# Another offset for the split weights in each of the seven stages that multiply h

## What is computed

```python
def swiglu(h, w_in, w_down):
    a, b = jnp.split(h @ w_in, 2, axis=-1)
    return (jax.nn.silu(a) * b) @ w_down
...
h = rms_norm(x, norm_g[layer, 0]) * (1.0 + scale) + shift
x = x + 0.5 * gate * swiglu(h, ffn_w_in[layer, 0], ffn_w_down[layer, 0])
h = rms_norm(x, norm_g[layer, 1]) * (1.0 + scale) + shift
y = diff_attention(h, ...) if layer == 0 else hgrn2(h, ...)      # both begin with h @ w, end with @ w_o
x = x + gate * y
h = rms_norm(x, norm_g[layer, 2]) * (1.0 + scale) + shift
x = x + 0.5 * gate * swiglu(h, ffn_w_in[layer, 1], ffn_w_down[layer, 1])
...
p = rmsnorm(x, norm_g_2) @ w_in_2                                # the last layer, one product of h for all mixers
```

## Time and profile before

| | |
|---|---|
| median of 3 runs | 2407.84 us (2407.11 to 2408.68) |
| span of the profiled execution | 2407.3 us |
| TensorE matmul, busy | 2373.9 us, 11034 instructions |
| TensorE weight load, busy | 1906.8 us, 11034 instructions |
| VectorE, busy | 1273.2 us |
| ScalarE, busy | 860.6 us |
| GpSimd, busy | 202.0 us |
| granted TensorE clock, mean | 0.994 of full speed |

### The profile page before, as it was taken

One profiled execution on the slowest core, in us unless ns is written; L12 is line 12 of the kernel. 1 busy time (PEld: TensorE's weight loads), 2 busy tenths in 40 slices (PEclk: granted clock), 3 DMA queues, 4 the chain that ended last, 5 costly groups with the idle time before them and its releaser, 6 DMA issues.

```text
span 2407.3 us, 30397 instructions
## 1 busy us (share of the span) xinstructions
PE 2373.9 (99%) x11034; PEld 1906.8 (79%) x11034; DVE 1273.2 (53%) x1953; ACT 860.6 (36%) x1320; POOL 202.0 (8%) x337
## 2 busy tenths in 40 slices
PE   7999999999999999999999999999999999999998
PEld 5888888677788888888888888888888888867766
DVE  6886334455678873343333355555533333469554
ACT  4222223566543222242222243344422222344443
POOL 1212000000001110000000013331000000120200
PEclk9999999999999999999999999999999999999999
DMA  8899332321259973223333321212233333242211
GB/s 279 277 287 294 111 96 72 98 62 53 70 168 288 289 230 108 86 79 96 96 99 108 90 79 54 62 53 79 86 97 96 96 111 96 69 97 62 62 53 53
DMA packets 420385, 285.27 MB, mean 119 GB/s; under 512 B 22690, under 2 KB 397788, under 8 KB 420304
## 3 DMA queue, kind: packets, MB, share of 16 engines
q1 hardware_dynamic: 397888, 207.64, 29.8%
q0 software_dynamic: 20896, 73.80, 9.3%
q10 hardware_dynamic: 1520, 2.77, 0.3%
HBM read 281.85 MB, written 6.72 MB: 120 GB/s over the span
## 4 chain that ended last, share of the span: by engine, by line
PE 92%; DVE 3%; ACT 2%; DMA 1%; issue 1%; SPq 1%; POOL 0%; ACTq 0%; DVEq 0%; POOLq 0%
PE bank L686 13%; PE bank L688 13%; PE bank L687 13%; PE bank L863 7%; PE bank L861 7%; PE bank L862 7%; PE bank L1530 4%; PE bank L1532 4%; PE bank L1531 4%; PE bank L1557 2%; PE bank L721 2%; PE bank L723 2%; PE bank L722 2%; PE bank L1179 1%; PE bank L1152 1%; PE bank L701 1%
## 5 line engine op out<-in xcount | busy, mean ns | idle before, releaser
L642 DVE TENSOR_TENSOR w_lo<-raw,w_hi 128x1024 fp32r<-128x1024 f32 (+1 forms) x331 | 434.0, 1311 | 423.9 <-ACT w_hi L623 418.4
L623 ACT ACTIVATE w_hi<-raw 128x1024 fp32r<-128x1024 f32 (+1 forms) x331 | 369.7, 1117 | 478.0 <-PE bank L688 243.2
L686 PE MATMUL bank<-h_hi,w_hi 128*128 128x512 f32 x1344 | 523.4, 389 | 1.6 <-DVE w_lo L642 1.6
L687 PE MATMUL bank<-h_lo,w_hi 128*128 128x512 f32 x1344 | 523.3, 389 | 0.0
L688 PE MATMUL bank<-h_hi,w_lo 128*128 128x512 f32 x1344 | 523.2, 389 | 0.0
L686 PEld LDWEIGHTS bank<-h_hi,w_hi 128*128 128x128 f32 x1344 | 252.4, 188 | 54.5 <-DVE w_lo L642 2.4
L687 PEld LDWEIGHTS bank<-h_lo,w_hi 128*128 128x128 f32 x1344 | 252.4, 188 | 52.4
L688 PEld LDWEIGHTS bank<-h_hi,w_lo 128*128 128x128 f32 x1344 | 252.4, 188 | 52.3
L861 PE MATMUL bank<-g_hi,w_hi 128*128 128x512 f32 x704 | 274.5, 390 | 0.0
L863 PE MATMUL bank<-g_hi,w_lo 128*128 128x512 f32 x704 | 274.1, 389 | 0.0
L862 PE MATMUL bank<-g_lo,w_hi 128*128 128x512 f32 x704 | 274.1, 389 | 0.0
(11 more groups left out here) (420 smaller groups left out, 3021.7 us busy)
## 6 DMA issues: line engine op xcount, KB each, us to landing
raw<-in_ffn_w_in SPq DMA_DIRECT2D x176, 512.0 KB, 3.9
ada<-in_ada_w POOLq DMA_DIRECT2D x128, 512.0 KB, 5.0
raw<-in_ffn_w_down SPq DMA_DIRECT2D x64, 704.0 KB, 4.6
raw<-in_hgrn_w_in SPq DMA_DIRECT2D x32, 512.0 KB, 4.0
raw<-in_attn_w_qkv SPq DMA_DIRECT2D x24, 512.0 KB, 3.8
raw<-in_w_in SPq DMA_DIRECT2D x22, 512.0 KB, 3.8
ada_first<-in_ada_w SPq DMA_DIRECT2D x16, 512.0 KB, 10.7
bias_scratch<-bias_lines POOLq DMA_DIRECT2D x14, 320.0 KB, 9.0
```

The source lines that it names most:

```text
L623: line(nc.scalar.activation(w_place(n, 0, k * P)[0], raw[:, n % 4, 0:k * P], ACT.Copy), hi_ready)
L642: line(nc.vector.tensor_tensor(lo, raw[:, n % 4, 0:k * P], hi.bitcast(F32), ALU.subtract), lo_ready)
L686: nc.tensor.matmul(out_ap, wh, xh, start=(k == 0), stop=False)
L687: nc.tensor.matmul(out_ap, wh, xl, start=False, stop=False)
```

## The change

Seven stages get a place of their own inside the slots. A table gives each an offset in elements: 16 (F0), 32 (F1), 48 (F2), 64 (F3), 80 (QKV), 96 (HIN), 112 (P2), that is 64, 128, 192, 256, 320, 384 and 448 bytes. Both halves of a block, in `w_hi` and in `w_lo`, are written and read that much further on; 1024 + 112 elements fit a slot of 1408. `raw`, h, the 16 blocks of each feed-forward that multiply g, and WO, HO and OUT stay where they are. No instruction is added, removed or moved on any engine, and no wait changes: the instruction lists of the two kernels read alike but for the line numbers.

```diff
+        PLACED = {"F0": (UP, 16), "F1": (UP, 32), "F2": (UP, 48), "F3": (UP, 64), "QKV": (24, 80), "HIN": (32, 96),
+                  "P2": (len(SECOND), 112)}
+
+        def w_cols(n, a, b):
+
+            at = sum(o for name, (count, o) in PLACED.items() if FIRST[name] <= n < FIRST[name] + count)
+            return slice(at + a, at + b)
 
         def w_place(n, a, b):
...
-            return w_hi[:, n % 2, a:b], w_lo[:, n % 2, a:b]
+            return w_hi[:, n % 2, w_cols(n, a, b)], w_lo[:, n % 2, w_cols(n, a, b)]
...
-                line(nc.scalar.activation(w_hi[:, n % 2, HALF:KD * P], raw[:, n % 4, HALF:KD * P], ACT.Copy), hi_ready)
+                line(nc.scalar.activation(w_hi[:, n % 2, w_cols(n, HALF, KD * P)], raw[:, n % 4, HALF:KD * P], ACT.Copy),
+                     hi_ready)
...
-                    nc.tensor.matmul(banks[b][:, :], w_hi[:, s, k * P:(k + 1) * P], xh, start=(k == 0), stop=False)
+                    nc.tensor.matmul(banks[b][:, :], w_hi[:, s, w_cols(n, k * P, (k + 1) * P)], xh, start=(k == 0),
+                                     stop=False)
...
-                wh, wl = w_hi[:, n % 2, k * P:(k + 1) * P], w_lo[:, n % 2, k * P:(k + 1) * P]
+                wh, wl = w_place(n, k * P, (k + 1) * P)
```

More of the change, by code:

```diff
@@ L573, in first_half_hi @@
             act.wait_ge(half_used, m + 1)
-            line(nc.scalar.activation(w_hi[:, n % 2, 0:HALF], raw[:, n % 4, 0:HALF], ACT.Copy), half_hi)
+            line(nc.scalar.activation(w_hi[:, n % 2, w_cols(n, 0, HALF)], raw[:, n % 4, 0:HALF], ACT.Copy), half_hi)
         def first_half_lo(dve, line, m):
@@ L579, in first_half_lo @@
             dve.wait_ge(half_hi, m + 1)
-            line(nc.vector.tensor_tensor(w_lo[:, n % 2, 0:HALF], raw[:, n % 4, 0:HALF],
-                                         w_hi[:, n % 2, 0:HALF].bitcast(F32), ALU.subtract), half_lo)
+            line(nc.vector.tensor_tensor(w_lo[:, n % 2, w_cols(n, 0, HALF)], raw[:, n % 4, 0:HALF],
+                                         w_hi[:, n % 2, w_cols(n, 0, HALF)].bitcast(F32), ALU.subtract), half_lo)
         IN_H = {FIRST["WO"] + 2: 0, FIRST["WO"] + 3: 1}
+        PLACED = {"F0": (UP, 16), "F1": (UP, 32), "F2": (UP, 48), "F3": (UP, 64), "QKV": (24, 80), "HIN": (32, 96),
[3 more added lines that the diff above has]
+            return slice(at + a, at + b)
         def w_place(n, a, b):
@@ L631, in split_lo @@
             if n in HALVED:
-                line(nc.vector.tensor_tensor(w_lo[:, n % 2, HALF:KD * P], raw[:, n % 4, HALF:KD * P],
-                                             w_hi[:, n % 2, HALF:KD * P].bitcast(F32), ALU.subtract), lo_ready)
+                line(nc.vector.tensor_tensor(w_lo[:, n % 2, w_cols(n, HALF, KD * P)], raw[:, n % 4, HALF:KD * P],
+                                             w_hi[:, n % 2, w_cols(n, HALF, KD * P)].bitcast(F32), ALU.subtract), lo_ready)
                 return
@@ L700, in product_pair @@
                     s = (n + b) % 2
-                    nc.tensor.matmul(banks[b][:, :], w_hi[:, s, k * P:(k + 1) * P], xh, start=(k == 0), stop=False)
-                    nc.tensor.matmul(banks[b][:, :], w_lo[:, s, k * P:(k + 1) * P], xh, start=False, stop=False)
+                    nc.tensor.matmul(banks[b][:, :], w_hi[:, s, w_cols(n, k * P, (k + 1) * P)], xh, start=(k == 0),
+                                     stop=False)
+                    nc.tensor.matmul(banks[b][:, :], w_lo[:, s, w_cols(n, k * P, (k + 1) * P)], xh, start=False,
+                                     stop=False)
                 pe.wait_ge(h_ready, KD * m + k + 1)
@@ L705, in product_pair @@
                     s = (n + b) % 2
-                    last = nc.tensor.matmul(banks[b][:, :], w_hi[:, s, k * P:(k + 1) * P], xl, start=False,
+                    last = nc.tensor.matmul(banks[b][:, :], w_hi[:, s, w_cols(n, k * P, (k + 1) * P)], xl, start=False,
                                             stop=(k == KD - 1))
@@ L735, in product_rows @@
                     xh, xl = h_hi[:, k, t * P:(t + 1) * P], h_lo[:, k, t * P:(t + 1) * P]
-                    wh = w_hi[:, n % 2, k * P:k * P + width]
-                    wl = w_lo[:, n % 2, k * P:k * P + width]
+                    wh, wl = w_place(n, k * P, k * P + width)
                     nc.tensor.matmul(o, xh, wh, start=(k == 0), stop=False)
@@ L1955, in out_part @@
                 hi, lo = y_pair(k)
-                wh, wl = w_hi[0:r, n % 2, k * P:(k + 1) * P], w_lo[0:r, n % 2, k * P:(k + 1) * P]
+                wh, wl = (w[0:r] for w in w_place(n, k * P, (k + 1) * P))
                 nc.tensor.matmul(B[j % 2][:, :], wh, hi[0:r], start=(m == 0), stop=False)
```

## The result

The changed kernel takes 2424.21 us (median of 3 runs, 2421.12 to 2426.09) against 2407.84 before: a ratio of 1.0063, 95% interval 1.0044 to 1.0083. It is slower, by 0.6% and clear of the interval, where no change was forecast. The span of its profiled execution is 2422.6 us, 15.3 more than before.

A forecast was written before the change was run, and what follows sets the result against it. TensorE was taken to bound the kernel through the pitch of its matmuls. Split 0, load 0 and pitch 0 on the profiled 2407.3 us, with the median 0.5 us above the span, gave 2407.8 us; range 2393 to 2437.

The forecast's parts named there:

- What bounds the kernel, and the scale: TensorE: time is matmul count times pitch; 6240 matmuls have moved weights, one ns on each pitch is 6.2 us.
- Writing the weights, 0: Split on ACT and DVE: another write address adds 0 to 0.5% of 1.236 us, hidden behind TensorE; taken as 0.
- loading them, 0: TensorE's weight load: 188 ns under a 227 ns pitch, no longer from another address; taken as 0.
- Weights and h at the same time, 0: TensorE reading weights and stream at a new distance within 512 bytes: settled pitch of 0.2267 us kept; taken as 0.
- The bounds: Limits on the pitch change of the 6240 matmuls: +0.0067 and -0.0067 us each, +41.6 and -41.6 us in all.
- Slower: h and weights fall out of step: Rival on TensorE's pitch: settled rhythm lost, about half the matmuls at 0.233 us, +22 us, 2430 us; chance 0.37.
- Faster: the present distance is itself the bad one: Rival on TensorE's pitch: 0.220 us in two feed-forwards, -14 us, 2394 us; in all seven stages 2366; chance 0.22.
- Mixed: Rival: the seven offsets act both ways and cancel to within 4.8 us; counted under no change, chance 0.41.
- The Trainium skill's rule: TensorE pitch of N / 2.4 GHz plus about 2.5 ns; would give 68 us less, 2339 us, placed among the rivals.
- The range: Kernel time expected to hold 8 in 10: 2393 to 2437 us, about 0.08 left above and 0.11 below.

The follow-up runs named there:

- e1: Changed kernel with weights 64 bytes further on in all seven stages; 2441.38 us, ratio 1.0143 to the kernel before.
- e2: Changed kernel with weights 256 bytes further on in all seven stages; 2408.06 us, ratio 1.0000 to the kernel before.
- e4: Changed kernel with weights of all seven stages and both halves of h 64 bytes further on; 2408.01 us, ratio 1.0000 to the kernel before.
- e5: Changed kernel with weight offsets 16, 32, 48, 8 bytes in F0 to F3, zero in QKV, HIN, P2; 2431.15 us against 2408.39 before.
- e7: Changed kernel with halves apart: w_lo alone moved 64, 128, 192 bytes in F0 to F2, w_hi alone 64 in F3; 2424.66 us.
- e8: Changed kernel using 64, 64, 32, 32 weight columns in `product`, F0 to F3, offsets 64, 0, 0, 64 bytes; 2428.18 us against 2408.39 before.
- e9: Changed kernel with h_lo moved 64 bytes, weight halves hi/lo at 0/64, 0/0, 64/64, 0/192 bytes in F0 to F3; 2434.83 us against 2409.24 before.

## Why the prediction was wrong

**What bounds the kernel, and the scale: right.** Nothing but the pitch of the 6240 matmuls changed, and the groups and waits stayed. The time follows from the pitch by stage, as worked out below.

**Writing the weights, 0; loading them, 0: right.** 1236, 1055 and 188 ns again. The transposes that were taken as rows for another address showed no difference, and rightly for the load itself.

**Weights and h at the same time, 0: this step failed.** The text took 0 because "the row nearest to a stage with one fixed offset is the settled stretch", where the distance does not change from matmul to matmul. It took constancy of the distance for the condition of the short pitch. e1 has one constant distance in each stage and runs at 233.3 ns; e2 and e4 have another one and run at 226.7. The value of the distance counts, modulo 256 bytes. Zero was a special case that the trace of before couldn't show as one, since every long stretch in it had it. For the measured value it was y8, the one tile with another distance (-192 bytes, so 64 modulo 256), that was near: 0.233 us. That row was read, put in the bounds, and set aside since its neighbours were as slow. Taken to the ns they were not quite: the three matmuls of y8 take 700 to 702 ns in seven of OUT's eight blocks, the three of the tile in front of it 691 to 697, and in the first block, where y8 takes 691, "every time" doesn't hold.

**The bounds held:** +6.67 ns was the step in F0, and no stage's pitch fell. By stage, 6.67 ns x 1056 = 7.0 us in F0 (the table has 6.2, since TensorE pauses less there than before), 5.7 x 1056 = 6.0 in F1, 2.2 x 1056 = 2.3 in F2, 0 in F3, together 15.3; QKV, HIN and P2 add 2.3, and the part ahead of F0, which the change does not touch, is 1.5 shorter (it lasts 39.1 to 41.0 us in the profiles of e1 to e4). The -0.9 of the last row says nothing: with no offset in P2 it lasts 313.9 to 314.9 us in e5 to e7 and 315.4 before.

**The rivals.** *Slower: h and weights fall out of step* was the case, at 2430 us for 2424. That its size came near was luck: it let the odd multiples of 64 bytes pay the full step and the even ones nothing. In fact 192 bytes cost a third of a step, 128 nearly a whole one, and 256 nothing. It also said that the broken stages would pay as the others do; they paid 2.3 us for 2016 matmuls, 1.1 ns each. That much of them is unsettled anyway is the likely reason, not shown. *Faster: the present distance is itself the bad one* falls: of twelve distances zero is the best for 512 columns. *Mixed* is answered by the windows: no feed-forward gained.

The Trainium skill's rule weighed there (page "TensorE: Matmul & The Clock Gate", section "Wait — 56ns, not 53.3ns?", 215.7 ns for 512 columns) was reached by no arrangement; the shortest pitch for 512 was 226.7, and for 496 columns 220.0. The same page, section "Step-by-step: what each phase is for", says that loading the next weights doesn't take read bandwidth from the running matmul. By that the size of the load would not matter to the pitch; in e8 it did, and in both directions (a quarter of the load: 231.7 for 226.7 ns at distance zero, 231.7 for 233.3 with 64 bytes). That the places of the two matter to each other, 226.7 against 233.3 ns, the page does not say.

**The range** held the time (2393 to 2437). The chance for slower, 0.37, was too low for a row that had been seen.

## What to carry to other kernels

In fp32r products where each matmul loads its own weights and streams 512 columns, allocate so that weight tiles and streamed tiles begin at the same place modulo 256 bytes, both halves of a split alike; here each of the eleven other distances tried cost 1.7 to 6.7 ns a matmul, up to 1.4% of the kernel, and halves placed apart 4.4 to 7.7. For other lengths of the stream measure it: with 480 columns 64 bytes were 0.7 ns better than zero. When something has a single value in the whole trace, the trace can't tell what other values cost; the one odd tile that differs is then the best row there is, and deserves the weight. Measure a pitch over a long window by its count, and look at single starts only for the rhythm.

## What the runs showed of the hardware

- The pitch of a settled run of fp32r matmuls closes on a beat of 6.67 ns, mostly within seven matmuls (fifteen in F1 of e9, 522 beats), for 384 to 512 columns and at every distance tried. In the kernel before, the starts of all settled stretches, taken modulo 6.667 ns, lie on one straight line over the whole execution (it drifts by 3.7 ns in 2.4 ms, no stretch is off by more than 0.3): the beat runs on through the pauses between them. In e4, with h and its weights 64 bytes further on and g and its weights not, the stretches with g lie on such a line and those with h on a second one, 1.7 ns off it, a quarter of a beat; with the weights of h moved by 256 bytes (e2) there is one line again. So the beat is tied to where the operands lie, and a quarter of it for a quarter of 256 bytes fits the 256 bytes after which the pitches repeat. What beats is not known.
- After other work a run of such matmuls needs up to ten to settle, at distance zero in the kernel before; until then single pitches go from 224 to 237 ns, 232 on the mean in the earlier trace rows.
- Fewer weight columns shortened the recorded load (188, 134 and 109 ns for 128, 64 and 32) and not, as a rule, the pitch: 32 instead of 128 gave 231.7 for 226.7 ns at distance zero, 231.7 for 233.3 with 64 bytes.
- 504 columns cost as much as 512, 496 cost 6.7 ns less or, in the last third of their stage, 3.3.
- One arrangement can have more than one settled rhythm (192 and 208 bytes; 496 columns at 0 and at 64 bytes), and changed it only at the start of a block.
- Open: why a distance picks its rhythm, what makes a run go from one to another, and whether the distance in a matmul's own pair or the change of start from one operand to the next breaks the good one.
